# Starting five products on half their features before the modulation is complete, and applying one RMS norm's scale to results instead of inputs

## The chip, the cores and the metric

The kernel runs on one core of one Trainium2 chip. The metric is the device time of one execution in microseconds (us). Each engine (TensorE, VectorE, ScalarE, GpSimd) executes its own instruction list strictly in the order in which it was written, and waits on semaphores that the others raise. In the rows they are PE (PEld for its weight loads), DVE, ACT and POOL, and SP is the engine that issues the DMA transfers.

## The reference, cut to what matters

Two transformer blocks over 256 tokens with 1024 features, in float32:

```python
c_act = silu(c)
mod = c_act @ w_ada + b_ada                  # 6 x 1024 columns
sh1, sc1, g1, sh2, sc2, g2 = split(mod, 6)
h = rms_norm(x, norm1_w) * (1 + sc1) + sh1                      # "N0"
p = h @ w_in                       # q, k, v, decays and betas ("ab"), z, gates, ...
...                                # gated delta rule over 8 heads, short conv, w_o
x = x + g1 * mix
h = rms_norm(x, norm2_w) * (1 + sc2) + sh2                      # "N1"
x = x + g2 * swiglu(h, w_ffn_in, w_ffn_out)
x = rms_norm(x, normf_w) * (1 + scf) + shf                      # "N2"
y = rms_norm(x, attn_norm)                                      # "N3"
q, k, v = y @ w_qkv                # then attention over 16 heads, w_o, x = x + ...
y = rms_norm(x, ffn_norm)          # "N4", then the gated MLP with a convolution
return rms_norm(x, final_norm)                                  # "N5"
```

`rms_norm` multiplies each token by 1/sqrt(mean of squares + eps) and each feature by a weight. Its first factor depends on the token only.

## The kernel before

Activations are kept transposed: 128 features on the partitions, 256 tokens on the free axis, eight such blocks (`kt` 0 to 7) for the 1024 features. For accuracy every operand of a big product is split into a high and a low part: `HH`, `HL` for the activation, `wh`, `wl` for the weights. A product ("q", "k", "q2", ...) yields 256 columns from 1024 features. Its weights come as one transfer of 1 MB into one of three `raw` buffers and are used as two units of 512 features. A unit is split by ACT (`hi`, line 1343: `wh` is a rounded copy) and DVE (`lo`, line 1696: `wl` is the rest), into one of five pairs of buffers. For each unit PE runs two slices (`t` 0 and 1, 128 output columns each) of twelve matmuls: eight on line 1002 (`HH` by `wh` and by `wl`) and four on line 1008 (`HL` by `wh`). The accumulators are PSUM banks, 0 to 2 in a ring `main`; banks 3 and 4 are a ring `misc` for small things; banks 5 to 7 are the streams of the delta rule.

A planner in Python writes one list, `plan`, and each engine's program is that list with what concerns it. `run(p)` emits a product's units. `tick()` advances every background task (a Python generator) by one step, once after almost every slice, so a task's instructions are dropped between slices, at fixed places. `until(...)` ticks until something has been emitted, before anything else is. `drain()` ticks until no task is left. How long anything takes plays no part in it.

The start. The modulation for N0 needs eight transfers of `ada` of 1 MB each: column blocks 2 and 0 (scale and shift of features 0 to 511), then 3 and 1 (features 512 to 1023), each in two parts. Blocks 0 and half of block 1 are computed on PE (`ada_rows`, line 1140), with a copy by ACT (line 1361) and four small matmuls ("turn", line 1149). The others are four fused multiply-adds on DVE (lines 1628, 1631), four transposes on PE ("red", line 1157) and a reduction on DVE (line 1643). N0 itself is a sum of squares on PE (lines 1167, 1168), Ln and Exp on ACT (lines 1328, 1330), then per block `scale` on DVE (line 1658), the high part on ACT (lines 1318 to 1324) and the low part on DVE (even `kt`, line 1668) or POOL (odd `kt`, line 1917). The first product starts after all eight `ada` transfers have been used. Each of q, k and v ends with a convolution: two ACT copies (line 1419) and six DVE instructions (line 1614), after which its bank is free. "ab" leads to the decays (lines 1454 to 1474 and 1780 to 1803), a chain between ACT, DVE and PE ("decays 3", line 1187). After a v product comes `silu` on ACT (line 1426), then `vturn` on PE (line 1195) two slices later, then two `l2sum` (line 1201).

The end of a block. `close` adds the last product to X, sums the last squares on PE (lines 1175 to 1179), makes R on ACT and runs 18 dummy matmuls (`warm`, line 1120). For N1 the scaled activation follows at once. Between "fo" and the attention there are two norms in a row: N2 is applied to X in place (`shift`: DVE line 1768, ACT line 1397), the squares of the result are summed on PE (`norm_sq`), R is made again, and only then come N3's `scale` and `parts` and the first product q2. The product q2 is evacuated by one ACT copy (line 1242).

Of the kernel before, what the change touches and what calls it, by code (L numbers as in the profile page):

```python
# [14 lines left out]
RAW = 3  # L15
HALF = 5
# [167 lines left out]
def _program(nc, a, out, ctx):  # L184
# [12 lines left out]
    d_raw = [signal(f"d_raw{i}", 16) for i in range(RAW)]  # L197
    d_dc, d_rb, d_u, d_out = (signal(n, 16) for n in ("d_dc", "d_rb", "d_u", "d_out"))
# [16 lines left out]
    w1c = sb("w1c", [128, 8])  # L215
    adr = sb("adr", [128, 4])
# [4 lines left out]
    sqs = [sb(f"sq{i}", [128, 512]) for i in range(3)]  # L221

# [38 lines left out]
    ffn.close()  # L261
    QA = sb("QA", [128, 8, T], where=phase)
# [35 lines left out]
    items, units, products = [], [], []  # L298

    def item(src, n, **kw):  # L300
        items.append(dict(src=src, n=n, i=len(items), units=[], **kw))
        return items[-1]

    def ada_item(b, kp, rows=False):
        item(a["ada"][b, :, 2048 * kp:2048 * (kp + 1)], 2048, ada=(b, kp), rows=rows)
# [6 lines left out]

    def product(kind, j, src, x, width=256, split=False, parts=((0, 2048),)):
        p = dict(p=len(products), kind=kind, j=j, x=x, split=split, width=width, units=[])
        products.append(p)
        p["items"] = []
        k0 = 0
        for at, n in parts:
            it = item(src[:, at:at + n], n, ada=None, rows=False)
            p["items"].append(it["i"])  # L320
            for c in range(0, n, 1024):
                m = min(1024, n - c)
                unit(it, p, c, m, m // width, width, k0)
                k0 += m // width
# [3 lines left out]
    for b, kp in ((2, 0), (0, 0), (2, 1), (0, 1), (3, 0), (1, 0), (3, 1), (1, 1)):  # L328
        ada_item(b, kp, rows=b == 0 or (b, kp) == (1, 0))
    for j in range(4):  # L330
        product("q", j, a["w_in"][j], (HH, HL, N0))
        if j == 0:
            product("ab", 0, a["wab"], (HH, HL, N0), width=128, parts=((0, 1024),))
        product("k", j, a["w_in"][4 + j], (HH, HL, N0))
        product("v", j, a["w_in"][8 + j], (HH, HL, N0))
# [46 lines left out]
    main, misc = Ring(range(3)), Ring((3, 4))  # L382
# [31 lines left out]
    for it in items:  # L414
        order += [("ada", it["i"])] if it["ada"] else [("u", u) for u in it["units"]]
# [425 lines left out]
    def startup():  # L841
        emit("begin")
        for i in range(8):
# [3 lines left out]
            if i == 2:  # L847
                direct_norm(N0)
# [1184 lines left out]
```

## Time and profile before

| | |
|---|---|
| median of 3 runs | 970.33 us (969.82 to 974.45) |
| the profiled execution | 974.01 us, of it 972.2 us span |
| PE busy | 926.5 us, 95% of the span |
| PE weight loads | 880.7 us, 91% |
| DVE busy | 667.2 us, 69% |
| ACT busy | 504.9 us, 52% |
| POOL busy | 65.2 us, 7% |
| mean granted clock of PE | 0.983 |

The span is the time from the first to the last instruction; the rest of an execution lies around it. A granted clock of 1.00 means that PE runs at its higher level (2.4 GHz), 0.50 at its lower (1.2 GHz). A busy PE can be a slow PE, so the clock has to be read beside the busy time.

### The profile page before, as it was taken

To read this page: it belongs to the slowest core of one execution; us is meant where nothing else is said; L and a number is where in the kernel's file an instruction comes from. 1 tells how busy PE (TensorE), PEld (TensorE's weight loads), DVE (VectorE), ACT (ScalarE), POOL (GpSimd) and SP (SyncE) were. 2 spreads that over 40 slices of the span, in tenths; PEclk is the share of its full clock that TensorE was granted. 3 is DMA by queue.
4 is the path that set the end of the run, shared out by engine and by line. 5 is a ranking of instruction groups with operands and counts; after the bars stand their busy time and mean duration, and the time that the engine had idled before them with its cause. 6 is when DMAs were issued, how large, how long until landed. Compare 5 with 4: busy or idle time off the path is not lost.

```text
span 972.2 us, 18558 instructions
## 1 busy us (share of the span) xinstructions
PE 926.5 (95%) x7996; PEld 880.7 (91%) x7996; DVE 667.2 (69%) x1113; ACT 504.9 (52%) x821; POOL 65.2 (7%) x91
## 2 busy tenths in 40 slices
PE   5789999999999999999989999989999999999997
PEld 2588888898899999989989999979998999999997
DVE  3876677557579986778758875465656677777643
ACT  2476666544344556455334444465565566665442
POOL 0100012011000000030000001010000300000001
PEclk9799999999999999999999999999999999999999
DMA  8743222232249985446898775515343345555631
GB/s 321 265 157 127 88 88 91 85 131 88 88 158 359 351 299 219 174 179 253 253 290 318 265 241 186 197 43 197 131 140 108 107 177 196 186 174 166 235 120 44
DMA packets 27681, 177.31 MB, mean 182 GB/s; under 512 B 2864, under 2 KB 5680, under 8 KB 7504
## 3 DMA queue, kind: packets, MB, share of 16 engines
q1 hardware_dynamic: 27600, 176.13, 51.5%
q8 instruction: 63, 1.03, 0.4%
q14 instruction: 18, 0.15, 0.0%
HBM read 174.29 MB, written 1.84 MB: 181 GB/s over the span
## 4 chain that ended last, share of the span: by engine, by line
PE 71%; DVE 12%; ACT 7%; DMA 7%; issue 2%; SPq 0%; DVEq 0%; ACTq 0%
PE ps L1002 38%; PE ps L1008 19%; DVE wl L1696 3%; DMA raw<-in_w_fi_dram 3%; DVE acc L1631 2%; ACT wh L1343 2%; PE ps L1000 2%; DMA raw<-in_ada_dram 1%; DMA raw<-in_w_rest_dram 1%; DVE tmp L1658 1%; PE ps L1046 1%; DMA raw<-in_w_sc_dram 1%; PE ps L1140 1%; PE ps L1054 1%; PE ps L1201 1%
## 5 line engine op out<-in xcount | busy, mean ns | idle before, releaser
L1002 PE MATMUL ps<-HH,wh 128*128 128x256 f32 x1480 | 388.0, 294 | 6.4 <-DVE wl L1696 5.5
L1696 DVE TENSOR_TENSOR wl<-raw,wh 128x1024 fp32r<-128x1024 f32 x265 | 321.4, 1233 | 97.2 <-ACT wh L1343 96.5
L1002 PE MATMUL ps<-HH,wl 128*128 128x256 f32 x1480 | 375.2, 285 | 0.0
L1343 ACT ACTIVATE wh<-raw 128x1024 fp32r<-128x1024 f32 x265 | 272.6, 1040 | 171.8 <-PE ps L1008 105.3
L1002 PEld LDWEIGHTS ps<-HH,wh 128*128 128x128 f32 x1480 | 287.1, 194 | 15.8 <-issue 8.0
L1002 PEld LDWEIGHTS ps<-HH,wl 128*128 128x128 f32 x1480 | 287.1, 194 | 2.1 <-issue 2.1
L1008 PE MATMUL ps<-HL,wh 128*128 128x256 f32 x1480 | 241.5, 286 | 2.6 <-DVE HL L1671 2.2
L1008 PEld LDWEIGHTS ps<-HL,wh 128*128 128x128 f32 x1480 | 207.3, 194 | 3.3 <-DVE HL L1671 2.6
L1002 PE MATMUL ps<-FH,wl 128*128 128x256 f32 x352 | 88.8, 285 | 0.0
L1002 PE MATMUL ps<-FH,wh 128*128 128x256 f32 x352 | 88.1, 279 | 0.0
L1631 DVE SCALAR_TENSOR_TENSOR acc<-raw,silc,acc 128x512 f32<-128x512 f32 x101 | 76.6, 758 | 8.4 <-DMA raw<-in_ada_dram 5.2
L1614 DVE SCALAR_TENSOR_TENSOR tmp<-ps,vec,tmp 128x255 f32<-128x255 f32 (+2 forms) x112 | 46.0, 474 | 31.1 <-ACT tmp L1413 29.3
L1002 PEld LDWEIGHTS ps<-FH,wh 128*128 128x128 f32 x352 | 66.9, 190 | 0.0
L1002 PEld LDWEIGHTS ps<-FH,wl 128*128 128x128 f32 x352 | 66.0, 187 | 0.0
L1008 PE MATMUL ps<-FL,wh 128*128 128x256 f32 x352 | 57.8, 282 | 0.0
L1922 POOL TENSOR_TENSOR sq<-sq 128x256 f32<-128x256 f32 x12 | 10.7, 888 | 597.7 <-ACT sq L1381 597.7
L1008 PEld LDWEIGHTS ps<-FL,wh 128*128 128x128 f32 x352 | 48.9, 188 | 0.0
L1504 ACT ACTIVATE FH<-tmp 128x512 fp32r<-128x512 f32 x22 | 13.9, 633 | 57.9 <-DVE tmp L1862 30.4
L1547 DVE TENSOR_TENSOR xz<-xz,ps 128x256 f32<-128x256 f32 x32 | 13.3, 420 | 29.3 <-PE ps L1057 28.8
L1002 PE MATMUL ps<-YH,wl 128*128 128x256 f32 x128 | 32.1, 284 | 0.0
L1002 PE MATMUL ps<-YH,wh 128*128 128x256 f32 x128 | 32.1, 281 | 0.0
L1413 ACT ACTIVATE tmp<-ps,vec 128x256 f32<-128x256 f32 x44 | 22.3, 556 | 15.6 <-PE ps L1008 15.6
(251 smaller groups left out, 1090.1 us busy)
## 6 DMA issues: line engine op xcount, KB each, us to landing
raw<-in_ada_dram SPq DMA_DIRECT2D x32, 1024.0 KB, 5.3
raw<-in_w_fi_dram SPq DMA_DIRECT2D x22, 1024.0 KB, 4.9
raw<-in_w_up_dram SPq DMA_DIRECT2D x22, 1024.0 KB, 4.8
raw<-in_w_rest_dram SPq DMA_DIRECT2D x20, 1024.0 KB, 4.8
raw<-in_w_in_dram SPq DMA_DIRECT2D x16, 1024.0 KB, 4.8
raw<-in_w_qkv_dram SPq DMA_DIRECT2D x12, 1024.0 KB, 4.8
raw<-in_w_o_dram SPq DMA_DIRECT2D x8, 1024.0 KB, 4.7
raw<-in_w_fo_dram SPq DMA_DIRECT2D x8, 1024.0 KB, 4.9
```

The source lines that it names most:

```text
L1000: e.matmul(o, x_hi[:, k0 + k, 128 * t:128 * t + 128], w[:, k, :], start=first and n + k == 0, **MM)
L1002: e.matmul(o, w[:, k, 128 * t:128 * t + 128], x_hi[:, k0 + k, :], start=first and n + k == 0, **MM)
L1008: ins = e.matmul(o, wh[:, k, 128 * t:128 * t + 128], x_lo[:, k0 + k, :], start=False, **MM)
L1046: ins = e.matmul(bank[g, 64 * c:64 * c + 64], S[f"d{n % 2}"][g, c, :], xz[g, 0, c, :], start=True, **MM)
L1343: e.activation(whl[u % HALF][0][:, 0:n], raw[i % RAW][:, c:c + n], ACT.Copy).then_inc(*a_hi.up(u))
L1413: e.activation(tmps[m][:, T * t:T * t + T], b[:, T * t:T * t + T], ACT.Identity, scale=v("conv2", 88 + ft), bias=v("conv2_b", ft)).then_in ...
L1504: e.activation(flat(dst, j), tmps[m][:, :], ACT.Copy).then_inc(*a_ev.up("hi", src, j))
L1547: e.tensor_tensor(xz4, xz4, b[:, 0:T], ALU.subtract).then_inc(*v_gdn.up("xz", h, n))
L1614: e.scalar_tensor_tensor(out=cv, in0=b[:, T * t:T * t + T - s], scalar=tap, in1=cv, op0=ALU.mult, op1=ALU.add).then_inc(*v_ev.up("conv", n ...
L1631: ins = e.scalar_tensor_tensor(out=acc_, in0=w, scalar=c, in1=acc_, op0=ALU.mult, op1=ALU.add)
L1696: e.tensor_tensor(wl[:, 0:n], raw[i % RAW][:, c:c + n], wh[:, 0:n].bitcast(F32), ALU.subtract).then_inc(*v_lo.up(u))
L1922: e.tensor_tensor(sqs[s][:, 0:T], sqs[s][:, 0:T], sqs[s][:, T:2 * T], ALU.add).then_inc(*g_norm.up(*(("sum", n, j) if j else ("part", n, 0))))
```

## The change

Part one, the start. The eight `ada` transfers get eight buffers of their own (in space that the mixer uses later), so they no longer wait for one another. Five products (q0, k0, v0, q1, k1) are opened in five banks (the ring `main` now holds 0, 1, 2, 5, 6) and their first halves, features 0 to 511, run as soon as the first half of the modulation is there. The rest of the modulation is computed between them. After it come the five second halves, then "ab", then v1 and the others. Banks 5 and 6 become streams once the convolutions of q1 and k1 have read them. The five transfers of a product are now ten of 512 KB. Eighteen dummy matmuls (`warm_up`) stand before the first half product.

Part two, N3. Its token factor R3 is applied to the results of q2, k2 and v2. The activation that goes into them is x' times attn_norm, with x' the output of N2, and is made directly from the X before N2, with weights `w1n` and shifts `shn`. In the background (`third_norm`) N2 is applied to X, squared and summed (POOL adds the partial sums), R3 is made, and for v2 is turned to a column (`norm_col`). q2 and k2 are evacuated on DVE with a multiplication by R3, v2 by two ACT copies.

```diff
+    ada_buf = [sb(f"ada{i}", [128, 2048], where=early) for i in range(EARLY_ADA)]
...
+    for n, (b, kp) in enumerate(((2, 0), (0, 0), (2, 1), (0, 1))):
+        ada_item(b, kp, rows=b == 0, early=n)
+    piece(*halved[0], 0, 1024)
+    for n, (b, kp) in enumerate(((3, 0), (1, 0), (3, 1), (1, 1))):
+        piece(*halved[n + 1], 0, 1024)
+        ada_item(b, kp, rows=(b, kp) == (1, 0), early=4 + n)
+    for p, w in halved:
+        piece(p, w, 1024, 1024)
+    product("ab", 0, a["wab"], (HH, HL, N0), width=128, parts=((0, 1024),))
...
-    main, misc = Ring(range(3)), Ring((3, 4))
+    main, misc = Ring((0, 1, 2, 5, 6)), Ring((3, 4))
...
+    def third_norm():
+        for i in range(4):
+            emit("shift", N2, i)
+            s, before = yield from take(sq)
+            emit("sq", N3, i, s, before, part[0] if i else None)
+            if i:
+                sq.give(part[0], g_norm, "part", N3, i)
+            part[:] = [s]
+            yield
+        yield
+        yield
+        bank, before = yield from take(misc)
+        emit("norm_sum", N3, part[0], bank, before)
+        sq.give(part[0], p_norm, "sum", N3)
+        emit("norm_r", N3, bank)
+        made.add("norm_r3")
+        misc.give(bank, a_norm, "ln", N3)
+        yield
+        bank, before = yield from take(misc)
+        emit("norm_col", N3, bank, before)
...
         elif kind in ("q2", "k2", "v2"):
-            emit("plain", p["p"], 0)
-            main.give(banks[0], a_ev, "plain", p["p"])
+            until("norm_r3" if kind != "v2" else "norm_col")
+            if kind == "v2":
+                emit("plain", p["p"], 0)
+                main.give(banks[0], a_ev, "plain", p["p"])
+            else:
+                emit("normed", p["p"], 0)
+                main.give(banks[0], v_ev, "normed", p["p"])
...
     def startup():
         emit("begin")
+        adas = [it["i"] for it in items if it["early"] is not None]
+        for i in adas[0:2]:
+            ada(i)
+        direct_norm(N0)
+        ada(adas[2])
+        drain()
+        ada(adas[3])
+        split_up_to(0)
+        low_of(0)
+        emit("warm_up")
+        drain()
+        emit("mod_scale", N0, 0)
+        for j in (0, 1):
+            scale(N0, j)
+        for j in (0, 1):
+            parts(N0, j)
+        for n, (p, _) in enumerate(halved):
+            split_up_to(n + 1)
+            low_of(n + 1)
+            open_banks(p)
+            for t in range(2):
+                emit("mm", p["units"][0], t)
+            if n < 4:
+                ada(adas[4 + n])
+            if n == 2:
+                drain()
+        drain()
+        emit("mod_scale", N0, 1)
+        for j in (2, 3):
+            scale(N0, j)
+        for j in (2, 3):
+            parts(N0, j)
+        emit("zero")
+        for p, _ in halved:
+            run_unit(p, 1)
+            close_product(p)
...
+            elif kind == "norm_sum":
+                _, n, s, b, before = ev
+                free(e, before)
+                g_norm.wait_ge(e, "part", n, 3)
+                e.matmul(psum[b][:, 0:T], ones, sqs[s][:, 0:T], start=True, **MM).then_inc(*p_norm.up("sum", n))
```

In the same diff, `mod_scale` of N1 and N2 is emitted before `close` instead of after it.

## Rows read from the trace of the kernel before

**Rows 1.** Windows: busy time per engine (instructions), clock, DMA share, GB/s

```profile
40.00:60.00 20.00, 17.80 (x123) 17.56 (x124) 16.32 (x29) 15.21 (x25) 2.33 (x2) 0.84 0.55 211
```

**Rows 2.** Timeline of PE in the start: start us, duration us

```profile
19.30 3.59 PE L1140 MATMUL ps<-raw,silc 128*1 128x512 f32 x8
22.83 0.66 PE L1157 MATMUL ps<-cst,acc 128*128 128x128 f32 x4
24.16 1.05 PE L1149 MATMUL ps<-cst,acc 1*128 1x1 f32 x8 [0.68 <-ACT acc L1361]
...
40.08 0.58 PE L1002 MATMUL ps<-HH,wh 128*128 128x256 f32 x1 [2.12 <-DVE wl L1696]
```

**Rows 3.** Timelines of ACT, DVE and POOL in the start

```profile
20.69 0.47 ACT L1328 ACTIVATE R<-ps,cst 128x256 f32<-128x256 f32 x1
...
25.32 0.68 DVE L1643 TENSOR_REDUCE adr<-ps 128x4 f32<-128x512 f32 x1
...
26.50 1.67 DVE L1658 SCALAR_TENSOR_TENSOR tmp<-X,w1c,R 128x256 f32<-128x256 f32 x4
...
29.69 1.00 POOL L1917 TENSOR_TENSOR HL<-tmp,HH 128x256 fp32r<-128x256 f32 x1 [0.52 <-ACT HH L1322]
```

**Rows 4.** Groups by line, page: busy, mean ns, idle before

```profile
L1696 DVE TENSOR_TENSOR wl<-raw,wh 128x1024 fp32r<-128x1024 f32 x265 | 321.4, 1233 | 97.2 <-ACT wh L1343 96.5
L1343 ACT ACTIVATE wh<-raw 128x1024 fp32r<-128x1024 f32 x265 | 272.6, 1040 | 171.8 <-PE ps L1008 105.3
```

**Rows 5.** DMA issues, 0 to 60 us: KB each, median us to landing

```profile
raw<-in_wab_dram SPq DMA_DIRECT2D x1, 512.0 KB, 3.4
```

**Rows 6.** Chain of waits, 60 to 73 us: start us, duration us

```profile
60.56 1.71 PE ps L1002 x8
...
67.39 0.84 ACT tmp L1419 x2
...
72.22 0.66 PE ps L1195 x4
```

**Rows 7.** Timeline of DVE, one convolution

```profile
68.27 2.43 DVE L1614 SCALAR_TENSOR_TENSOR tmp<-ps,vec,tmp 128x255 f32<-128x255 f32 x6 [1.82 <-ACT tmp L1419]
```

**Rows 8.** What PE waited for, 40 to 260 us: total, times, longest

```profile
PE ps L1195 <- ACT tmp L1426: 3.3, 4, 2.0
PE ps L1187 <- DVE G L1790: 2.1, 1, 2.1
```

**Rows 9.** Windows of 6 us behind two waits of PE, columns as in rows 1

```profile
72.00:78.00 6.00, 5.78 (x30) 4.85 (x31) 0.96 (x1) 2.63 (x5) 0.00 (x0) 0.72 0.49 175
...
638.00:644.00 6.00, 4.52 (x13) 3.75 (x14) 3.14 (x7) 3.51 (x9) 0.00 (x0) 0.72 0.01 3
```

**Rows 10.** Chain of waits around N1 and around N2 with N3

```profile
431.67 0.42 ACT R L1330
...
436.93 0.95 PE ps L1002 x8
...
636.14 0.42 ACT R L1330
...
650.50 0.95 PE ps L1002 x8
...
654.80 0.96 PE ps L1002 x8
```

**Rows 11.** Timelines of ACT, PE and POOL around the norms

```profile
438.22 0.42 ACT L1322 ACTIVATE HH<-tmp 128x256 fp32r<-128x256 f32 x1
...
635.43 2.17 PE L1120 MATMUL ps<-cst 128*128 128x128 f32 x18
...
639.24 1.75 ACT L1397 ACTIVATE X<-X,modc 128x256 f32<-128x256 f32 x4
640.90 0.61 ACT L1369 ACTIVATE sq<-X 128x512 f32<-128x512 f32 x1
...
425.39 0.88 POOL L1922 TENSOR_TENSOR sq<-sq 128x256 f32<-128x256 f32 x1 [3.19 <-ACT sq L1381]
```

More of the change, by code:

```diff
@@ L311, in unit, with open_product, piece @@
         p["units"].append(u)
+    def open_product(kind, j, x, width=256, split=False):
+        p = dict(p=len(products), kind=kind, j=j, x=x, split=split, width=width, units=[], items=[], k=0)
+        products.append(p)
+        return p
+    def piece(p, src, at, n):
+        it = item(src[:, at:at + n], n, ada=None, rows=False)
+        p["items"].append(it["i"])
+        for c in range(0, n, 1024):
+            m = min(1024, n - c)
+            unit(it, p, c, m, m // p["width"], p["width"], p["k"])
+            p["k"] += m // p["width"]
@@ L313, in product @@
     def product(kind, j, src, x, width=256, split=False, parts=((0, 2048),)):
[L314 to L317, printed above, removed]
+        p = open_product(kind, j, x, width, split)
         for at, n in parts:
[L319 to L324, printed above, removed]
+            piece(p, src, at, n)
@@ L326, in _program @@
     down = ((0, 2048), (2048, 2048), (4096, 1536))
     N0, N1, N2, N3, N4, N5 = range(6)
[L328 to L335, printed above, removed]
+    qkv = {"q": 0, "k": 4, "v": 8}
@@ L414, in _program @@
     for it in items:
-        order += [("ada", it["i"])] if it["ada"] else [("u", u) for u in it["units"]]
+        if it["early"] is None:
+            order += [("ada", it["i"])] if it["ada"] else [("u", u) for u in it["units"]]
     def split_up_to(u):
@@ L545, in conv_qkv @@
         emit("conv", p["p"], 0)
-        main.give(bank, v_ev, "conv", p["p"], 3, 1)
+        give_main(bank, v_ev, "conv", p["p"], 3, 1)
         yield
@@ L701, in attend @@
         made.add(("oa", h))
+    def third_norm():
[18 more added lines that the diff above has]
+        emit("norm_col", N3, bank, before)
+        made.add("norm_col")
+        misc.give(bank, a_norm, "col")
+        misc.order[:] = [b for b in misc.order if b[0] == 3]
     norm_of = {"wo": N1, "fo": N2, "wo2": N4, "dn": N5}
@@ L770, in after @@
                 misc.give(4, v_att, "lo", dict(open_heads)[0])
+            if n == N1:
+                mod(4)
+                mod(3)
+                emit("mod_scale", n, 0)
+            elif n == N2:
+                mod(7)
+                mod(6)
+                emit("mod_scale", n, 0)
             close(n, p)
@@ L1158, in tensor_engine @@
                 ins.then_inc(*p_misc.up("red", blk))
+            elif kind == "warm_up":
+                for _ in range(WARM):
+                    e.matmul(psum[7][:, 0:128], ones, eye, start=True, **MM)
             elif kind == "norm_sq":
```

244 lines of the change are left out of this document (129 added, 115 removed).

## The prediction

> **What bounds the kernel now.** I read the page first. PE is busy for 926.5 of 972.2 us, so there are 45.7 us in which it does nothing, and its mean granted clock of 0.983 says that it also works slowly for a while. A change can only win there. The windows of 20 us say where: the worst stretches are the first 80 us, in which PE is often idle and its clock is below 1.00 [rows 1], and the place between the first block and the attention. Everywhere else PE is busy for 18 to 20 of 20 us at full clock. Then I read the start engine by engine and the chain of waits around the two places [rows 2, 3, 6, 10]. Three things are to be seen. The first big product starts at 40.08 [rows 2]. From 60.56 to 67.39 the four slices of v0 run, and then PE waits until 72.22 for the silu behind it [rows 6]. And between the R of N2 (ready at 636.56) and the second slice of q2 (650.50) lie 13.9 us, where at N1 the same two points lie 4.84 us apart (432.09 and 436.93) [rows 10]: the second norm costs 9.1 us of PE.
>
> A slice of twelve matmuls takes 1.43 us: three lie between 650.50 and 654.80 [rows 10]. A unit is two slices, 2.87.
>
> **The clock, as a price.** Behind a wait of PE of about 2 us comes a stretch at the lower level of 1.2 GHz. The mean clock of 0.72 over 6 us, behind the wait for silu and behind the one for the squares [rows 9], means 3.4 us at 0.50 and the rest at 1.00, so that 1.7 us of work are lost each time. The sum below goes by this 1.7. The Trainium skill (TensorE: Matmul & The Clock Gate, "HAM oscillation — how this bites in real kernels") speaks against this change: a TensorE that stands idle between bursts is throttled again and pays anew each time; the trace agrees, with its 1.7 us.
>
> **Part one, up to the first half products.** The transfers no longer wait, but they don't set this stretch. PE's list does, and its order is new. After the sums of squares (the rows of block 0 follow at 19.30 [rows 2]) come the four transposes of block 2. `misc` has two banks: one holds the rows, the other is the norm's, and is free only when its Ln has been read, at 21.16 [rows 3]. So PE waits 1.9 us there, which it doesn't now. Then: transposes 0.66, rows 3.59, turn 1.05 [rows 2], and between rows and turn eighteen dummies, 2.17 [rows 11]. That is 21.16 + 7.5 = 28.6, where the turn ends at 25.21 now. DVE then needs one addition and w1c; the reduction of 0.68 that lies between now [rows 3] is already done. The first `scale` starts at about 29.1 instead of 26.50 [rows 3]. If the wait of 1.9 us brings the low clock, add 1.7: 30.8. The low parts on POOL end 4.2 us after `scale` starts (26.50 to 30.69 [rows 3]), at 33.3 to 35.0, and behind the last of them the first slice; the second is through at 34.9 to 36.6.
>
> **The half products.** PE's list is now q... unit, unit, rows, unit, turn, transposes, unit, unit, transposes: four more units 11.5, rows 3.6, turn 1.05, transposes twice 1.3, together 17.4 us, until 52.3 to 54.0. DVE has the five splits of 1.23 [rows 4] and three `ada` sums beside it, about as long. Then the reduction, w1c and `scale` (1.0), POOL's low parts (4.2), and the second slice of q0's second half ends at 59.1 to 60.8. By then twelve slices are done. Now, ten slices are done at 60.56 [rows 6]. So the new order is ahead by two slices and up to 1.5 us, 2.7 to 4.3 us; I take 3.5. It is not the 14.4 us of the five half products, because the modulation takes as much longer as they take on the same engines: PE would be through with it at 40 now, and at 54 then.
>
> **The second half products, and what they owe.** At 60.56 the decays and the convolution of q0 are behind the kernel now. In the new order they are ahead of it. Each of the five second halves takes PE 2.87 us, and DVE one convolution (2.43 [rows 7]) and one split (1.23 [rows 4]), 3.66: after five, DVE is 4 us late. PE doesn't wait for the convolutions themselves, as the banks suffice. It waits in `vturn`, which stands at a fixed place two slices behind v0: now it comes 4.8 us after the copy of v0 starts and costs a wait of 2.0 [rows 6, 8]. With DVE late by three convolutions of the five I take 5.0, so 3.0 more. The decays' chain, whose wait of 2.1 us [rows 8] lies before 60.56 now, lies after it then: 2.1. The low clock follows both as now, so I count it once in each and not in the difference. The transfers moved are ten of 512 KB in place of five of 1 MB; each takes 3.4 us to land [rows 5], and each waits until the split three pieces earlier has emptied its buffer. k1's second piece is asked for when the third half's split has run, its `hi` stands before the copy of q0 on ACT, and so the first convolution may start a microsecond later; that is within the 3.0. SP's issues of `ada` are moved before everything and wait for nothing. The memsets move to where DVE is busy, under 1 us, hidden while PE has units split. Sum of part one: -3.5 + 3.0 + 2.1 = +1.6, slower. The bounds: if DVE is not late and the decays hide, -4.3, and if the present two waits vanish as well (2.0 + 2.1, and 1.7 twice), -11.8; if the low clock hits the first chain and DVE's delay costs its own stretch too, -2.7 + 5.1 + 1.7 = +4.1.
>
> **Part two, N3.** What goes: the norm between R and q2. If q2 follows R of N2 as `fg` follows at N1, its second slice starts at 636.56 + 4.84 = 641.4, and q2's four slices end at 645.7 instead of 654.80: 9.1 us gained. What comes: `until("norm_r3")` stands behind q2's last slice, and it makes the planner emit `norm_sum` there, before any slice of k2. PE's list is fixed, so PE can't go on with k2 while R3 is on its way. And R3 is late, through ACT. At N1 ACT is through with the high parts at 438.64, 6.55 us after R (432.09) [rows 10, 11], so here at 643.1. Then in its list come eight shifts (four in 1.75 [rows 11]: 3.5), four squares (0.61 [rows 11], less their overlap: 2.2) and two splits for coming units (1.04 each [rows 4]): 7.7, so 650.8. POOL adds twice, 0.88 each [rows 11]: 652.6. PE sums (0.6 to 1.0), ACT does Ln and Exp (0.47 and 0.42 [rows 3, 10]), and PE must turn R3 to a column before k2, because `norm_col` is emitted with the next tick: four small matmuls, half of the turn's 1.05 at full clock [rows 2], all of it at half. k2 starts at 655.4, not at 654.80: +0.6. PE has then waited nearly 9 us with one sum between, so k2 runs into the low clock: +1.7. The copy of q2 moves from ACT to DVE (one instruction over 512 columns; nearest the split of 1024 in 1.23, so 0.6 to 0.7), which waits for nothing else by then. Attention starts behind k2 as before, with 0.7 on DVE for 0.6 on ACT. v2's two copies on ACT lie beside the slices. DVE gets 6 us more in the 100 us of attention, where PE is the busy one; price 0, and if that cover failed, up to 1 us. Sum of part two: +2.3. Bounds: -9.1, if R3 were ready when q2 ends; +4.5, if POOL and ACT are each a microsecond slower and the low stretch is met twice.
>
> `mod_scale` before `close` puts 0.16 us of DVE before N1's last addition: +0.1. At N2 it lies in DVE's idle time.
>
> **Sum.** 1.6 + 2.3 + 0.1 = +4.0 on the profiled execution, 974.01 to 978.0. That execution is 3.7 us above the median of the runs shown, with the same program; the difference is carried to the median: 970.33 + 4.0 = 974.3.
>
> **The rivals.** *A: the start pays, N3 doesn't.* The late DVE costs nothing, because silu and the decays find other slices over them, and the low stretches behind the present waits go: -4 to -12, middle -8, with +2.3: 964.6. For it: twelve slices against ten, and PE idle for 2 us twice in the start now. Against it: the fixed places of `vturn` and "decays 3". Chance 0.2. *B: R3 comes in time,* or the stall is half of what I say: the two splits or shifts are not in ACT's way. Then part two gives -9 to -4, say -6, and the whole 966.0 with part one as forecast. For it: 9.1 us are really there. Against it: the 7.7 us of ACT are bound by rows, and they start 2.6 us before q2 ends. Chance 0.1. *C, the slower case, a low stretch behind every wait:* every new wait (21.16, the mod between the halves, `vturn`, the decays, R3) is followed by a low stretch. In this kernel that would be three more than I count, 3 x 1.7 = 5.1: 979.4. It decides against "no change" from one stretch more on. For it: each wait of about 2 us in the start has such a stretch behind it now [rows 9]. Against it: where half products follow with small gaps only, as at N1, the clock stayed. Chance 0.3. (It is the rule of the Trainium skill, TensorE: Matmul & The Clock Gate, "HAM oscillation — how this bites in real kernels", taken at its strongest.) My forecast, both waits as worked out: 0.4.
>
> **The numbers.** 974.3 is the forecast. With a noise of some 2 us around each, the cases give a range of 964 to 981. About 0.5% (4.9 us) is what a measurement of this kernel can tell from no change: below 965.5 is faster, above 975.2 slower. A gives faster in half of its chance or more, B in a third, and a surplus for waits that I believe in and that don't come: 0.22. C gives slower nearly whole, the forecast in a quarter of its chance: 0.37. Same: 0.41. The forecast's own range is 970 to 978.
>
> **What the profile after would show.** The first `scale` near 29 to 31, and PE waiting for the Ln before the transposes. The first second half near 54 to 56. A wait of PE of about 5 us in `vturn` and of 2 in "decays 3", with a clock under 1.00 behind both. q2's last slice 9 us after R of N2 and `norm_sum` 7 us later, its wait ended by POOL; then k2 at a clock near 0.5. If `norm_sum` waits under 2 us, part two is wrong by the difference. If the waits of `vturn` and "decays 3" are together under 4 us, part one is wrong. The attention's stretches and all behind it should have the same length as before.

## The result, and the profile after

The changed kernel takes 991.15 us, the median of four runs (988.72 to 991.84), beside 971.17 us for the kernel before on the same chip. The ratio is 1.0182, 95% interval 1.0136 to 1.0229: slower by 1.4% to 2.3%. The forecast was 974.3 us in a range of 964 to 981.

Four marks divide the kernel: the eighteen dummy matmuls in `close`, once for each of N1, N2, N4 and N5 (before, N2's are at 635.43 [rows 11]). Here are their starts, before and after, in us, with a fifth, the first evacuation of k2:

```
                     before   after   later by   added in the stretch
N1                   430.96   442.42   11.46      11.5   start, recurrence, first block
N2                   635.43   647.15   11.72       0.3
first KA written     660.6    677.2    16.6        4.9   third norm, q2, k2
N4                   767.14   787.79   20.65       4.1   attention, w_o2
N5                   964.55   982.32   17.77      -2.9   last block
```

The marks are those of one execution each, and good to some 2 us either way. Two kernels below run the same instructions up to N1, with the same distances between their tiles, and have N1 at 426.90 and 429.66, where the kernel before has it at 430.96.

So there are four questions: what part one lost by N1, what the third norm cost, why the attention got longer, and why the last block got shorter without any edit to it.

**The start.** In the timeline of PE after, up to 60 us (start us, duration us), the steps that the prediction named can be found:

```profile
19.88 0.66 PE L1236 MATMUL ps<-cst,acc 128*128 128x128 f32 x4 [1.85 <-ACT R L1422]
20.47 3.59 PE L1219 MATMUL ps<-ada,silc 128*1 128x512 f32 x8
...
26.20 1.05 PE L1228 MATMUL ps<-cst,acc 1*128 1x1 f32 x8
28.79 0.36 PE L1079 MATMUL ps<-HH,wh 128*128 128x256 f32 x1 [1.54 <-ACT HH L1417]
...
54.92 0.35 PE L1079 MATMUL ps<-HH,wh 128*128 128x256 f32 x1 [2.21 <-ACT HH L1417]
```

The first product starts at 28.79 where it started at 40.08 [rows 2], PE waits 1.85 us for Ln's bank, and the first second half starts at 54.92. But the windows behind it show the other side (columns as in rows 1); the first two are the kernel before, the last two the changed one:

```profile
60.00:80.00 20.00, 18.01 (x120) 16.63 (x119) 10.64 (x22) 12.03 (x20) 0.00 (x0) 0.84 0.30 106
80.00:100.00 20.00, 18.67 (x176) 17.23 (x176) 18.66 (x41) 14.10 (x28) 2.67 (x6) 1.00 0.29 107
```

```profile
60.00:80.00 20.00, 14.42 (x97) 13.24 (x95) 15.22 (x30) 12.48 (x20) 0.00 (x0) 0.84 0.62 225
80.00:100.00 20.00, 14.95 (x95) 13.47 (x94) 10.25 (x22) 13.83 (x24) 0.00 (x0) 0.84 0.30 106
```

PE is idle for 10.6 of these 40 us instead of 3.3, and in 80 to 100 its clock is 0.84 instead of 1.00. Two things stand there. The first is transfers. In the timelines of the DMA queue and of ACT after:

```profile
36.87 22.57 SPq L1043 DMA_DIRECT2D raw<-in_w_in_dram  x5
60.24 0.33 SPq L1043 DMA_DIRECT2D raw<-in_wab_dram  x1
```

```profile
62.97 1.06 ACT L1437 ACTIVATE wh<-raw 128x1024 fp32r<-128x1024 f32 x1 [3.26 <-DMA raw<-in_w_in_dram]
63.94 0.82 ACT L1517 ACTIVATE QT<-ps,vec 128x256 f32<-128x256 f32 x2
65.89 1.06 ACT L1437 ACTIVATE wh<-raw 128x1024 fp32r<-128x1024 f32 x1 [1.13 <-DMA raw<-in_wab_dram]
...
69.09 1.06 ACT L1437 ACTIVATE wh<-raw 128x1024 fp32r<-128x1024 f32 x1 [1.41 <-DMA raw<-in_w_in_dram]
```

The ring `raw` has three slots. Half of a product's weights, 512 KB, takes a whole slot, so the five second pieces are issued one by one over 22.6 us, each when a split has emptied a slot. ACT has the splits of coming units ahead of the copies of q0, k0 and v0, waits 5.8 us in all for transfers, and the copies wait behind it. The second thing is what PE waited for, 0 to 310 us, after (total, times, longest):

```profile
PE ps L1287 <- ACT tmp L1524: 5.9, 2, 5.6
PE ps L1279 <- issue: 5.1, 1, 5.1
...
PE ps L1161 <- DVE lc L1662: 3.3, 2, 2.3
PE ps L1164 <- DVE v L1666: 2.0, 2, 1.4
```

The first row is `vturn` behind silu (2.0 at the longest before [rows 8]), the second "decays 3" (2.1 before [rows 8]). The view names no releaser for the second; the timeline has it start 0.1 us after DVE's scan of G ends.

**The third norm.** In the timeline of PE after, and the window around it:

```profile
656.89 0.64 PE L1085 MATMUL ps<-HL,wh 128*128 128x256 f32 x4
665.45 1.19 PE L1262 MATMUL ps<-sq,cst 128*128 128x256 f32 x2 [7.92 <-POOL sq L2039]
667.65 1.01 PE L1256 MATMUL ps<-cst,R 1*128 1x1 f32 x4 [1.01 <-ACT R L1424]
668.59 0.58 PE L1079 MATMUL ps<-HH,wh 128*128 128x256 f32 x1
...
676.48 0.64 PE L1085 MATMUL ps<-HL,wh 128*128 128x256 f32 x4
```

```profile
660.00:680.00 20.00, 12.66 (x73) 11.43 (x74) 7.78 (x16) 8.24 (x15) 4.68 (x6) 0.66 0.24 81
```

q2 is done at 657.4, PE waits 7.92 us for POOL's sums of squares with k2 queued behind, and k2 then runs slowly.

**The attention.** What PE waited for, first in the kernel before (628 to 770 us), then after (640 to 790):

```profile
PE ps L1108 <- DVE ap L1592: 2.1, 6, 0.4
```

```profile
PE ps L1187 <- DVE ap L1690: 4.3, 6, 1.3
PE ps L1256 <- ACT R L1424: 1.0, 1, 1.0
PE ps L1181 <- DVE KA L1923: 0.9, 1, 0.9
```

### The profile page after: what moved, and what is told of

The parts are those of the page before. It is cut to its first block, busy times and chain, and to the rows that moved or that the text cites. A ratio compares the mean times of both kernels' runs of the same rounds, so it can differ in the third digit from the quotient of the medians.

```text
span 990.1 us, 18583 instructions
## 1 busy us (share of the span) xinstructions
PE 926.6 (94%) x7986; PEld 881.1 (89%) x7986; DVE 673.2 (68%) x1121; ACT 508.6 (51%) x825; POOL 69.5 (7%) x98
## 4 chain that ended last, share of the span: by engine, by line
PE 77%; DVE 9%; ACT 6%; DMA 4%; issue 1%; POOL 0%; DVEq 0%; ACTq 0%
PE ps L1079 43%; PE ps L1085 21%; DMA raw<-in_w_fi_dram 3%; DVE wl L1800 2%; PE ps L1077 2%; ACT wh L1437 2%; DVE tmp L1758 1%; PE ps L1125 1%; PE ps L1133 1%; PE ps L1136 1%; DMA raw<-in_w_in_dram 1%; PE ps L1083 1%; DVE tmp L1945 1%; PE ps L1236 1%; PE ps L1293 0%
## 5 line engine op out<-in xcount | busy, mean ns | idle before, releaser
L1079 PE MATMUL ps<-HH,wh 128*128 128x256 f32 x1480 | 394.6, 298 | 10.0 <-ACT HH L1417 4.1
L1079 PE MATMUL ps<-HH,wl 128*128 128x256 f32 x1480 | 379.7, 287 | 0.0
L1079 PEld LDWEIGHTS ps<-HH,wh 128*128 128x128 f32 x1480 | 290.7, 196 | 21.3 <-issue 12.9
L1079 PEld LDWEIGHTS ps<-HH,wl 128*128 128x128 f32 x1480 | 291.0, 197 | 2.2 <-issue 2.2
L1085 PEld LDWEIGHTS ps<-HL,wh 128*128 128x128 f32 x1480 | 209.4, 196 | 2.7 <-DVE HL L1770 1.3
L1079 PE MATMUL ps<-FH,wl 128*128 128x256 f32 x352 | 86.9, 280 | 0.0
L1079 PE MATMUL ps<-FH,wh 128*128 128x256 f32 x352 | 86.9, 280 | 0.0
L1729 DVE SCALAR_TENSOR_TENSOR acc<-raw,silc,acc 128x512 f32<-128x512 f32 x84 | 64.0, 761 | 3.1 <-DMA raw<-in_ada_dram 0.6
L2034 POOL TENSOR_TENSOR sq<-sq 128x256 f32<-128x256 f32 x16 | 14.1, 883 | 600.6 <-ACT sq L1479 600.6
```

The costliest lines, as they stand in the source:

```text
L1079: e.matmul(o, w[:, k, 128 * t:128 * t + 128], x_hi[:, k0 + k, :], start=first and n + k == 0, **MM)
L1085: ins = e.matmul(o, wh[:, k, 128 * t:128 * t + 128], x_lo[:, k0 + k, :], start=False, **MM)
L1729: ins = e.scalar_tensor_tensor(out=acc_, in0=w, scalar=c, in1=acc_, op0=ALU.mult, op1=ALU.add)
L2034: e.tensor_tensor(sqs[s][:, 0:T], sqs[s][:, 0:T], sqs[s][:, T:2 * T], ALU.add).then_inc(*g_norm.up(*(("sum", n, j) if j else ("part", n, 0))))
```

## The experiments

Times are medians; ratios are against the kernel before on the same chip, with 95% intervals. "N1 at" is the start of the dummies of N1 in the profiled run.

### Each part alone

Part one alone is the change without `third_norm`, R3, the two new small tiles and the evacuations on DVE; part two alone is the reverse.

> The kernel before with part one alone. Theory (the two parts add, and part one carries what the trace shows lost by the first modulated norm's end, 11.5 us): +10 to +13 us, 981 to 983, with the dummy matmuls of N1 near 442.4 and those of N3's place near 646.9. Rival (the start costs what was forecast, and most of the loss at the start is a clock or table effect that comes with part two): under +5 us. Matmul pitch in the products of w_ffn_out and of the last down product stays at 1.44 us for a slice, since no tile behind HL moves.

> The kernel before with part two alone. Theory: +4.8 us until the first k2 product is evacuated (norm_sum waits for the POOL additions with k2 behind it on TensorE), +4.1 us in the attention (q2 and k2 evacuated by VectorE ahead of the softmax), -2.9 us in the two products that read FH and FL, together +6 us, 977. Rival (the stall at norm_sum is only a follow-up of the late start): near +2 us or less. N1's landmark stays within 0.3 us of before.

Part one alone: 987.45 us, ratio 1.0145 (1.0121 to 1.0170), N1 at 442.96. Part two alone: 978.18 us, 1.0057 (1.0034 to 1.0080), N1 at 428.52. The parts add: 1.45% and 0.57% against 1.82% together. N1 of part two should have stayed within 0.3 us and is 2.4 earlier, without an edit that bears on it: that is the scatter of the marks. By the marks, part two has 30.1 us from N2 to the first KA (before 25.2), 110.6 from there to N4 (106.5), and 2.9 us less in the last block. Part one has 26.6 and 106.6 in the first two, and 1.5 us less in the last block, where neither its instructions nor its tiles differ from before; the next section returns to this. The waits of part two are those of the changed kernel, 7.9 for POOL's squares and 4.3 for the softmax. Both rivals fall.

### The last block: 64 bytes

```diff
     w1c = sb("w1c", [128, 8])
+    pad = sb("pad", [128, 16])
```

> The kernel before with one unused tile of 64 bytes per partition where the changed kernel has its two new small tiles; no instruction differs. Theory (the matmul's pitch depends on where its operands lie in SBUF, and FH and FL have moved by 64 bytes): slices of the products of FH and FL take 1.41 us where they took 1.44, and the kernel is 2.9 us shorter. Rival (the pitch changed for another reason, such as the clock or the DMA's load): no difference, within 0.5 us, slices 1.44.

968.25 us, 0.9951 (0.9933 to 0.9969): 3.0 to 6.5 us faster, with not one instruction changed. Groups of PE's instructions, before and then with the 64 bytes (busy us, mean ns):

```profile
L1002 PE MATMUL ps<-FH,wl 128*128 128x256 f32 x352 | 88.8, 285 | 0.0
L1002 PE MATMUL ps<-FH,wh 128*128 128x256 f32 x352 | 88.1, 279 | 0.0
L1008 PE MATMUL ps<-FL,wh 128*128 128x256 f32 x352 | 57.8, 282 | 0.0
```

```profile
L1003 PE MATMUL ps<-FH,wh 128*128 128x256 f32 x352 | 86.9, 280 | 0.0
L1003 PE MATMUL ps<-FH,wl 128*128 128x256 f32 x352 | 86.9, 280 | 0.0
L1009 PE MATMUL ps<-FL,wh 128*128 128x256 f32 x352 | 56.9, 280 | 0.0
```

From start to start a slice takes 1.408 us instead of 1.440, and each of the two blocks has 44 such slices (`w_ffn_out` in the first, the last down product in the last). The theory holds for the pitch. `w1n` and `shn` of part two are together 64 bytes per partition, ahead of FH and FL, and the changed kernel has the same 1.408.

But 44 slices at 0.032 us are 1.4 us, and the last block was 2.9 shorter. The other 1.5 are the clock. Windows of 20 us that hold the norm behind N4, the kernel before and then the changed one (columns as in rows 1):

```profile
765.00:785.00 20.00, 18.74 (x132) 17.57 (x131) 13.18 (x21) 12.05 (x22) 3.60 (x4) 0.91 0.25 87
```

```profile
785.00:805.00 20.00, 18.73 (x145) 17.57 (x144) 13.82 (x23) 13.02 (x23) 3.64 (x5) 1.00 0.34 124
```

PE is idle as long in both, and 0.09 of 20 us, 1.8 us of work, are lost to the clock in the first alone. The last block takes 197.4 us in the kernel before; 195.9 in part one, with a clock of 1.00 there; 194.5 in part two, with 1.00 and the 64 bytes. With the 64 bytes and a clock of 0.91, as in the run with `norm_sum` behind k2 below, it takes 196.0. So the tile gave the changed kernel 1.4 us in this block, and the 1.5 belong to the one execution of the kernel before that was profiled.

### Whose place counts

All tiles moved by 64 bytes (the same 64 bytes ahead of `raw`), and HH and HL moved by 100 bytes with 28 more behind them:

```diff
+    pad0 = sb("pad0", [128, 25])
     HH = sb("HH", [128, 8, T], F32R)
     HL = sb("HL", [128, 8, T], F32R)
+    pad1 = sb("pad1", [128, 7])
```

> The kernel before with everything moved by 64 bytes per partition, the weight tiles too, so that all distances between tiles stay. Theory (the place of FH itself counts): the products of FH and FL go at 1.41 us a slice as in the run with the 64-byte tile behind the weights, about -4 us, and those of HH may change too. Rival (the distance between FH and the weight tiles counts): as before, within 1 us.

> The kernel before with HH and HL moved by 100 bytes per partition (28 bytes behind them, so that FH and FL keep their places modulo 128). Theory (the pitch of the products depends on where the moving operand starts): slices of the products of HH and HL fall from 1.44 us to 1.41, 740 of them, -20 us at the most and -10 if only a part of them responds. Rival (only the products of FH and FL respond, or the layout that counts is another): within 1 us.

All moved: 972.36 us, 0.9995 (0.9979 to 1.0012), slices as before, 1.44. So it isn't FH's own address; what is left is its distance from the tiles ahead of it, and of these PE reads the weight tiles beside it.

This run shows something else by the way. Its instructions are those of the kernel before, and so is its wait for silu; the clock behind it is not. Its row of waits (40 to 260 us) and its window, to be set beside the 0.84 of the kernel before:

```profile
PE ps L1196 <- ACT tmp L1427: 3.3, 4, 2.0
60.00:80.00 20.00, 18.01 (x141) 16.85 (x140) 13.89 (x26) 14.90 (x24) 0.00 (x0) 1.00 0.28 107
```

The same 2.0 us of waiting brought a stretch at the lower level in one execution and none in the other, and it is part of the scatter of N1 (426.90 here).

HH moved: 967.26 us, 0.9937 (0.9916 to 0.9958), 4 to 8 us faster; slices of HH take 1.42 to 1.43 us. They respond, by half of what was hoped for. A third layout put HH and HL 356 bytes on, and FH with FL 576:

```diff
+    pad0 = sb("pad0", [128, 89])
     HH = sb("HH", [128, 8, T], F32R)
     HL = sb("HL", [128, 8, T], F32R)
+    pad1 = sb("pad1", [128, 55])
```

> The kernel before with unused tiles ahead of HH (356 bytes) and behind HL (220 bytes), so that HH and HL lie, modulo 512, where FH and FL lay in the run with the 64-byte tile. Theory (the distance from the weight tiles modulo 512 sets the pitch): slices of HH at 1.41 us as well as those of FH, 370 + 88 slices at 0.03 us or more, -12 to -18 us, near 958. Rival (only a few per cent of the HH products respond, as with 100 bytes): -6 to -9 us. Second rival (the residue modulo 512 is not what counts): no gain for HH.

960.78 us, 0.9866 (0.9840 to 0.9892): 10 to 16 us faster than the kernel before, and the best version of all. HH stays at 1.42, FH in `w_ffn_out` takes 1.41, and the last down product 1.36, as its timeline shows (start us):

```profile
910.72 0.62 PE L1010 MATMUL ps<-FL,wh 128*128 128x256 f32 x4
912.08 0.62 PE L1010 MATMUL ps<-FL,wh 128*128 128x256 f32 x4
913.44 0.62 PE L1010 MATMUL ps<-FL,wh 128*128 128x256 f32 x4
```

The residue modulo 512 isn't the rule, since HH and FH have the same here and differ. What all five layouts share is the distance modulo 128: where it is 0 or 36 bytes a slice takes 1.44 us, where it is 100 bytes 1.36 to 1.43. These five tried only three remainders, and what decides inside the span stays open.

### The third norm: norm_sum behind k2

```diff
-            until("norm_r3" if kind != "v2" else "norm_col")
+            begin(evacuate(p))    # a task that waits for norm_r3 or norm_col
...
-        yield
-        yield
+        for _ in range(4):
+            yield
         bank, before = yield from take(misc)
         emit("norm_sum", N3, part[0], bank, before)
```

> Part two alone, with norm_sum behind the first k2 product instead of behind the first q2, norm_col behind the third quarter of v2, and the three evacuations as tasks that wait for the rows. Theory (TensorE stood 7.9 us at norm_sum with k2 queued behind it): the stall goes and the low clock behind it, 7 to 10 us under part two alone, 968 to 971; the attention's loss of 4 us stays. Rival (the softmax needs q2 and k2, whose evacuation still waits for the row, so the wait moves to the first attention products): under 3 us gained.

971.09 us, 0.9987 (0.9968 to 1.0006), against 1.0057 for part two alone: 7 us gained, the lower end of what the theory gave. From N2 to the first KA it takes 22.5 us, where part two alone takes 30.1 and the kernel before 25.2. What PE waited for from 628 us on:

```profile
PE ps L1137 <- DVE ap L1637: 4.3, 6, 1.3
PE ps L1209 <- POOL sq L1986: 2.1, 1, 2.1
PE ps L1131 <- DVE KA L1870: 1.5, 1, 1.5
```

The wait at `norm_sum` falls from 7.9 to 2.1 us. So the stall was the order in PE's list, as the theory says. The attention's 4 us remain: mended in this way part two gains 2.7 us at the norm and pays 4.3 in the attention, and it takes the faster slices of FH and of the product behind the attention to bring it level with before.

### The attention: q2 and k2 evacuated by DVE

```diff
-                emit("plain", p["p"], 0)
-                main.give(banks[0], a_ev, "plain", p["p"])
+                emit("normed", p["p"], 0)
+                main.give(banks[0], v_ev, "normed", p["p"])
...
+                e.scalar_tensor_tensor(out=..., in0=psum[...], scalar=w, in1=ones..., op0=ALU.mult, op1=ALU.mult)
```

> The kernel before with the evacuation of q2 and k2 moved from ScalarE to VectorE and nothing else (a multiplication by 0.125 or 1.0, one instruction of the same shape). Theory (each evacuation stands in VectorE's list ahead of the softmax of four heads, and TensorE waits for that): +3 to +5 us, with TensorE's waits for the softmax's p near 4.3 us in six instead of 2.1. Rival (the evacuation is hidden, and the attention's loss comes from the later order of k2 or from the clock): within 1 us.

977.33 us, 1.0042 (1.0023 to 1.0062), 2 to 6 us slower. From the first KA (660.3) to N4 (770.20) it takes 109.9 us instead of 106.5, and:

```profile
PE ps L1112 <- DVE ap L1592: 3.9, 6, 1.3
```

The edit alone makes 3.4 us. Eight evacuations of 0.69 us stand in DVE's list ahead of the softmax of the heads before them, and PE waits for that softmax: 1.8 us more than before in the row above, and 2.5 more idle time in the whole stretch. The changed kernel's 4.1 us hold two more things that nearly cancel. Its clock is 0.91 in 705 to 725 us, 1.8 us lost, where the kernel before and this run have 1.00. And the 16 slices of the product behind the attention take 1.36 us each instead of 1.44, 1.3 us less, since its operand has moved as well (by `w1n`, `shn` and `r3c`, 72 bytes).

### The start: transfers

The five second pieces get buffers of their own behind the `ada` buffers, so no ring slot is waited for, and the memsets of `inv` move behind them:

```diff
+    ada_buf += [sb(f"second{i}", [128, 1024], where=early) for i in range(EARLY_W)]
...
-    for p, w in halved:
-        piece(p, w, 1024, 1024)
+    for n, (p, w) in enumerate(halved):
+        piece(p, w, 1024, 1024, early=EARLY_ADA + n)
```

> Part one alone, with the five second pieces loaded into buffers of their own, so that they wait for no slot of the raw ring and the pieces behind them come earlier (the memsets of the recurrence's tiles stand behind the second halves). Theory (the raw ring of three slots is what part one lost most to: ScalarE's waits of 3.3, 1.1 and 1.4 us for transfers, with the conv copies queued behind them): N1's dummy matmuls 6 to 9 us earlier than in the run with part one alone, 434 to 437. Rival (the loss is the order of the conv work and of the decays behind five products, and the transfers hide in it): within 2 us of part one alone, near 442.

982.37 us, 1.0097 (1.0073 to 1.0120); N1 at 439.69, 3.3 us before that of part one alone. Neither 6 to 9 nor under 2: the ring is one cause, the smaller. (The ratios give 0.5% between the two runs, some 4.7 us, and their intervals just fail to overlap.) How far each kernel had got can be counted: the matmuls of HH and HL that the trace holds by a given time, summed over windows. One that lies across the edge of two windows is counted in both, in each kernel alike.

```
until us           40    60    80   100   120   140   200   240   260   300
before              0   122   236   344   425   513   758   932  1018  1298
part one alone     48   141   236   320   406   492   736   912   994  1198
second pieces own  49   147   269   342   425   508   756   931  1003  1219
```

At 60 us part one is 19 matmuls ahead (about 2.3 us at 0.12 each; 3.5 were forecast), at 100 us 24 behind. With buffers of their own it is level from 100 to 240 us, and loses some 75 matmuls, about 9 us, from 240 to 300. That is the end of the recurrence. DVE and PE there, second pieces in their own buffers (two timelines):

```profile
239.24 0.61 DVE L1594 SCALAR_TENSOR_TENSOR l<-ps,GC,dec 128x128 f32<-128x128 f32 x2 [1.25 <-PE ps L1088]
...
243.56 0.50 DVE L1603 TENSOR_TENSOR xz<-xz,cst 128x128 f32<-128x128 f32 x1
243.98 1.21 DVE L1758 TENSOR_TENSOR wl<-raw,wh 128x1024 fp32r<-128x1024 f32 x1
245.11 0.34 DVE L1626 SCALAR_TENSOR_TENSOR lc<-ps,neg,V 128x128 f32<-128x128 f32 x1
```

```profile
245.51 0.80 PE L1141 MATMUL ps<-lc,inv 128*128 128x128 f32 x2 [2.33 <-DVE lc L1626]
```

The heads run as pairs and a third alone. The first pair starts at 95.4 us on DVE (before 85.5), the pairs behind it at 163.9 and 234.4 (153.5 and 224.2): 10 us late each time. The single head starts as before, at 119.2 and 192.2 (191.8). So the last pair's opening now falls on the last steps of the single head, and seems to hold them up.

### The start: the place of the decays

Three orders of the product ab, which feeds the decays (in part one it is last, behind the five second halves):

```diff
+    ab = open_product("ab", 0, (HH, HL, N0), 128)
...
+        if n == 0:      # n == 2 for the third place
+            piece(ab, a["wab"], 0, 1024)
```

> Part one alone, with the product ab (the decays' input) behind q0's second half instead of behind the five second halves. Theory (the first head's recurrence starts on VectorE at 100.1 us, 14.6 us later than before, and its last wait is the decays': ab stood behind four more second halves): the recurrence starts near 93 us, where v0's norm allows it, and N1's dummy matmuls come 4 to 7 us before those of part one alone, 436 to 439. Rival (the late transfers and ScalarE's queue set the start of the recurrence, or TensorE has enough other work until then): within 2 us of 443.

> Part one alone, with the second pieces in buffers of their own and ab behind q0's second half. Theory (the ring and the place of ab are two separate losses): N1's dummy matmuls 8 to 10 us before part one alone, 433 to 435, and the kernel 4 us behind before or less. Rival (the two losses are one queue, so that mending the second adds nothing to the 3.3 us of the first): near 439.

> Part one alone, second pieces in buffers of their own, and ab behind v0's second half (third) instead of last or second. Theory (the first pair of heads must start on time, since the pairs follow each other at a fixed distance of some 69 us, and its start is set by what comes last of v0's norm and the decays; with ab last it was the decays at 95.2 us, with ab second it was v0's chain, pushed back by the decays' work): the decays are done near 85 us, the first dec at 87 to 90 us on VectorE (before: 85.5), N1's dummy matmuls at 432 to 435 (before: 431.0), the kernel within 4 us of before. Rival (the place of the recurrence in TensorE's list, behind 233 rows of main products where it was behind 197, sets the start by itself): the first dec at 94 or later and N1 near 440.

ab second: 987.16 us, 1.0122 (1.0091 to 1.0152), N1 at 445.64. Second, with the buffers: 984.36 us, 1.0119 (1.0085 to 1.0153), N1 at 439.99. Third, with the buffers: 989.7 us, 1.0191 (1.0162 to 1.0221), N1 at 449.48. (In the last two the memset of `G40` stays ahead of the second halves, because the decays need it.) Of the three theories none held, of the rivals only the second run's. The decays came when they should; the first pair did not follow. The rows of DVE for the decays' last step and the first pair, part one alone and then with ab second:

```profile
99.78 0.17 DVE L1862 TENSOR_SCALAR neg<-neg 128x16 f32<-128x16 f32 x1 [2.53 <-ACT neg L1533]
100.05 0.61 DVE L1583 SCALAR_TENSOR_TENSOR dec<-ps,ngc,cst 128x128 f32<-128x128 f32 x2
```

```profile
85.60 0.17 DVE L1867 TENSOR_SCALAR neg<-neg 128x16 f32<-128x16 f32 x1 [0.30 <-ACT neg L1538]
102.82 0.61 DVE L1588 SCALAR_TENSOR_TENSOR dec<-ps,ngc,cst 128x128 f32<-128x128 f32 x2 [0.51 <-PE ps L1084]
```

What the pair waited for instead can be read from DVE's rows. In the kernel before and in all five versions of the start it begins with the later of two things: the decays' last step, or the normalising of k0 by DVE that follows the product v0 (`KT` by `sq`), and within 1.1 us of it. In part one the normalising ends at 92.5 us and the decays at 100.0; with ab second at 102.3 and 85.8; with ab third at 90.9 and 86.9. Each order brings one forward and pushes the other back.

With ab second PE waits 6.6 us for a convolution on DVE: the five half products hold all five banks of `main`, so ab needs q0's, and q0's convolution has to be through with it. With ab third the first pair starts at 92.0, earlier than in any other version of part one, and N1 is the latest of all: PE waits 14.0 us in four `vturn`s. My theory that the first pair's start sets the loss is refuted by this run. Every order pays in another wait.

The reverse, the kernel before with ab behind q1:

```diff
-        if j == 0:
+        if j == 1:
             product("ab", 0, a["wab"], (HH, HL, N0), width=128, parts=((0, 1024),))
```

> The kernel before with the product ab behind q1 instead of behind q0, nothing else: the decays come late, the recurrence keeps its place behind 197 rows. Theory (a late first pair of heads is carried to the recurrence's end, and there TensorE runs out of cover): the first dec 3 to 8 us later than 85.5, the pairs behind it late by the same, N1's dummy matmuls 2 to 6 us later than 431.0, TensorE idle 2 to 4 us more between 240 and 300 us. Rival (a late recurrence is caught up, because TensorE is full between 100 and 240 us either way): N1 within 1 us of before.

978.1 us, 1.0071 (1.0044 to 1.0098), 4 to 10 us slower; N1 at 434.66, 3.7 us later than before and 5.0 and 7.8 later than the two kernels with the same start. The pairs start at 88.7, 157.8 and 228.4, 3.2 to 4.3 us late. The wait that appears:

```profile
PE ps L1187 <- issue: 5.0, 1, 5.0
```

It is the same 5 us as in part one, where 2.1 stood before [rows 8]. The time of the first pair and N1 are as the theory said; the place of the loss is not: PE is idle no more than before between 240 and 300 us (0.63 us both times). It is lost at 80 to 100, in the wait and at a clock of 0.74.

### All mends together

> The changed kernel with all three mends: second pieces in buffers of their own, ab behind q0's second half, norm_sum behind the first k2. Theory (the losses are the raw ring, the place of ab, the stall at norm_sum and the evacuations on VectorE, and they add): 991 less 9 less 7, 974 to 977. Rival (the parts hold each other up, through the clock or the queues): 981 or more.

982.12 us, 1.0085 (1.0061 to 1.0108): the changed kernel with the buffers, ab second and `norm_sum` late (here `third_norm` also waits until both banks of `misc` are free). That is about 9 us better than the changed kernel, where 14 to 17 were expected, and the rival's figure; N1 is at 440.78, from N2 to N4 133.7 us (before 131.7). It is still 6 to 10 us behind the kernel before.

## Why the prediction was wrong

On the profiled executions the change adds 17.8 us (991.84 against 974.01), and +4.0 was forecast. The sum had +1.7 for the start where 11.5 came, +2.3 for the third norm where 4.9 came, and 0 for the attention where 4.1 came. Point by point:

**Up to the first second half: right.** PE's wait for Ln is 1.85 us (1.9), the rows 3.59, the turn ends at 27.3 (28.6), the first `scale` is at 27.61 (29.1), and the first second half starts at 54.92 (54 to 56). The lead, forecast at 2.7 to 4.3 us, is 2.3 at 60 us, a little short.

**The transfers: the step that failed.** "The transfers moved are ten of 512 KB in place of five of 1 MB ... that is within the 3.0." I followed one piece, k1's, and not the ring behind it. Three slots hold three halves where they held three wholes, so the ring runs half as far ahead. ACT waited 3.26, 1.13 and 1.41 us, ahead of the three copies. Buffers of their own gave back 3.3 us at N1.

**The waits in vturn and "decays 3".** "So 3.0 more" for `vturn`: it waited 5.6 instead of 2.0, 3.6 more, nearly right (2.0 once the transfers were out of the way). "2.1" for the decays, assumed to be the wait of before in another place: it was 5.1. In the trace after, the silu, the norm behind v0 and the decays share ACT between 71 and 93 us, with a table load of 1.28 us at each change between them; before, the decays had ACT to themselves but for the splits. Putting them late in the kernel before brought the same wait of 5.0 and made it 4 to 10 us slower.

**"The low clock follows both as now, so I count it once in each and not in the difference": failed too.** In 60 to 100 us PE's idle time and its lost clock (idle, plus length times one minus the clock) are 10.6 + 6.4 = 17.0 us, against 3.3 + 3.2 = 6.5. The lost clock alone is 3.2 us of the 10.5. (The reckoning counts idle time at the lower level twice, so it is an upper bound.) From 0 to 430 us it gives 6.8 us more idle time and 5.1 more lost clock, 11.9 together, where N1 came 11.5 later: 5.3 were gained up to 60 us, and 10.5, 1.8 and 4.8 lost in 60 to 100, 100 to 240 and 240 to 430. The price itself, 1.7 us behind every wait of 2 us, was less firm than rows 9 made it look, since the kernel with all tiles moved had the same wait of 2.0 at full clock.

**What I didn't see at all: the recurrence.** Some 5 us are lost between 240 and 430 us by the same reckoning (4.3 + 1.7 against 1.2). The cause, as far as the trace shows it, is that DVE's list has the pair's steps ahead of the single head's. I had stopped at the wait nearest to the edit. That this order is what costs there is read from the trace of the run with the buffers, not tested alone, and the rearrangements show only that the loss moves. How the remaining 8 us of part one divide between the decays' wait and the recurrence's order stays open.

**Part two's norm: the mechanism was right, two terms were small.** q2 ended 9.1 us behind R, `norm_sum` waited 7.92 us for POOL, and k2 ran slowly, as foretold. k2 started 21.4 us behind the mark of N2, where 20.0 were forecast and 19.4 are the rows of before [rows 10, 11]. Its four slices took 8.4 us (668.59 to 677.0) instead of 5.7: the low clock cost 2.7 us there and not "+1.7". Together 4.7 against 2.3.

**"price 0, and if that cover failed, up to 1 us": failed.** The attention lost 4.1 us, and the evacuations on DVE alone cost 3.4. I priced them by DVE's total time, where "PE is the busy one"; PE waited for DVE six times there already before the change.

**The last block.** "The attention's stretches and all behind it should have the same length as before": the attention didn't, and the last block was 2.9 us shorter. 1.4 of it come from the place of a tile, which no step had. The other 1.5 are a stretch at the lower clock in the kernel before, which the prediction missed: "Everywhere else PE is busy for 18 to 20 of 20 us at full clock" does not hold, its clock is 0.91 in 760 to 780 us and in 500 to 520, where PE is busy for 17.0 us. "PE waits until 72.22" was loose too: from 67.4 on it works for 2.8 us and waits for 2.0; the sum used the 2.0.

The rivals: C, a low stretch behind every wait, was on the right side with 979.4 and too small; A and B did not occur. The Trainium skill's rule (TensorE: Matmul & The Clock Gate, "HAM oscillation — how this bites in real kernels") warned in the right direction: a clock of 0.84 behind the new waits at 80 to 100 us and 0.66 around k2 agree with it. It would not have given the size alone, since up to 430 us less than half of the loss is clock, and the rest is waiting. My bounds added up to +8.7 at the most, because each came from the size of a stall that existed before, where new ones were made.

## What to carry to other kernels

When a transfer is cut in two, follow the whole ring with half the bytes in each slot, and the queue of the engine that empties it, and not one piece. When an instruction moves to another engine, ask what stands behind it in that engine's list and who waits for that; an engine at a moderate share of busy time can still be the one that is waited for. And when every engine's order is fixed, bringing one product forward delays others by the same count: name the dependent chain that is now late and follow it to where it ends, far behind the edit.

## What the hardware showed that I had not expected

The pitch of the fp32 matmuls depends on where the moving operand lies relative to the weights. HH and HL lie at a multiple of 128 bytes from the weight tiles in the kernel before, FH and FL 36 bytes past one (summed from the sizes of the tiles). With the same instructions, a slice of twelve takes 1.44 us at distances of 0 and 36 bytes modulo 128, and 1.36 to 1.43 at 100 bytes. 64 bytes of unused SBUF made this kernel 0.5% faster and 576, placed as above, 1.3%. A small new tile can so hide or feign the effect of an edit, as `w1n` and `shn` did here with 1.4 us in each block's down product.

The same wait does not always bring the lower clock. Two kernels with the same instructions waited 2.0 us for silu; the clock in 60 to 80 us was 0.84 in one execution and 1.00 in the other. A difference of 1.5 us between two single profiles can be this alone, as it was in the last block.
